# An eighth weight chunk by seven block products, the last mix's preparation moved ahead, and one ring of banks, in a float32 kernel on one Trainium2 core

## The reference, cut to what matters

```
u = rms_norm(x, norm_in_g)
proj = u @ w_in                      # 1024 x 4096: 16 chunks of 256 columns
pool_x, pool_z, m_x, m_z = split(proj)   # chunks 0-3, 4-7, 8-11, 12-15
pooled_g = window_mean(pool_x[g], w) - pool_x[g]     # w = 2, 4, 8, 16
mixed_g = pooled_g @ pool_w[g]                       # 256 x 256
y_pool = mixed * pool_scale * silu(pool_z)
h = x + y_pool @ w_out[:1024] + y_m @ w_out[1024:]
```

## Time and profile before

| | |
|---|---|
| median of 3 runs | 1152.65 us (1152.45 to 1152.68) |
| profiled execution, time | 1152.89 us |
| its span | 1151.1 us |
| PE busy | 1140.1 us, 99% of the span |
| DVE, ACT, POOL busy | 63%, 34%, 42% |
| granted TensorE clock | 0.998 |

### The profile page before, as it was taken

The page is one execution under the profiler, slowest core; times in us unless marked ns, Lnnn a source line. Parts: engine busy times, 40 slices in busy tenths (PEclk is TensorE's granted clock), DMA queues, the critical chain, the costliest instruction groups (busy, mean ns, idle before and its releaser), DMA issues.

```text
span 1151.1 us, 17423 instructions
## 1 busy us (share of the span) xinstructions
PE 1140.1 (99%) x6515; PEld 931.5 (81%) x6515; DVE 727.4 (63%) x1335; ACT 386.5 (34%) x758; POOL 482.7 (42%) x475
## 2 busy tenths in 40 slices
PE   9999999999999999999999999999999999999997
PEld 6888887888888887788888888889888887777786
DVE  5944545467344894467777964894698434556668
ACT  7432233222000022546574621341111134553422
POOL 2356655332223241244666765304224224455534
PEclk9999999999999999999999999999999999999999
DMA  8323343213325522101114241232111220142113
GB/s 245 120 64 121 99 146 104 90 51 114 110 67 193 209 69 97 52 24 28 47 42 161 64 175 45 102 124 74 43 50 38 66 71 1 38 149 101 44 40 138
DMA packets 84230, 104.07 MB, mean 90 GB/s; under 512 B 14258, under 2 KB 61578, under 8 KB 82995
## 3 DMA queue, kind: packets, MB, share of 16 engines
q1 hardware_dynamic: 76422, 99.21, 25.9%
q10 hardware_dynamic: 7724, 3.74, 1.2%
HBM read 80.35 MB, written 24.17 MB: 91 GB/s over the span
## 4 chain that ended last, share of the span: by engine, by line
PE 86%; POOL 8%; DMA 3%; ACT 1%; issue 1%; DVE 1%; POOLq 0%; DVEq 0%; ACTq 0%
PE bank L1064 20%; PE bank L1066 19%; PE bank L1065 19%; PE bank L1394 4%; POOL wlo L845 4%; PE bank L1369 4%; DMA wraw<-in_w_in 3%; PE wide L1385 2%; PE wide L1594 2%; PE bank L1333 1%; PE bank L1322 1%; PE bank L1310 1%; PE wide L1066 1%; PE wide L1065 1%; PE wide L1064 1%
## 5 line engine op out<-in xcount | busy, mean ns | idle before, releaser
L804 POOL CAST whi<-wraw 128x2048 fp32r<-128x2048 f32 x24 | 48.0, 1999 | 334.6 <-PE bank L1066 267.3
L1064 PE MATMUL bank<-x_hi,wlo 128*128 128x512 f32 x312 | 123.6, 396 | 0.0
L1064 PE MATMUL bank<-u_hi,wlo 128*128 128x512 f32 x308 | 120.6, 392 | 1.4 <-POOL wlo L808 1.4
L1066 PE MATMUL bank<-x_hi,whi 128*128 128x512 f32 x312 | 121.7, 390 | 0.0
L1065 PE MATMUL bank<-x_lo,whi 128*128 128x512 f32 x312 | 121.7, 390 | 0.0
L1066 PE MATMUL bank<-u_hi,whi 128*128 128x512 f32 x308 | 120.0, 390 | 0.0
L1065 PE MATMUL bank<-u_lo,whi 128*128 128x512 f32 x308 | 120.0, 390 | 0.0
L808 POOL TENSOR_TENSOR wlo<-wraw,whi 128x2048 fp32r<-128x2048 f32 x21 | 99.8, 4750 | 2.1 <-ACT whi L2908 0.5
L1064 PEld LDWEIGHTS bank<-x_hi,wlo 128*128 128x128 f32 x312 | 58.6, 188 | 16.1 <-issue 4.3
L1008 POOL TENSOR_SCALAR sp<-sp,rcx 128x384 f32<-128x384 f32 (+1 forms) x64 | 37.9, 606 | 76.4 <-DVE rcx L2392 76.3
L1064 PEld LDWEIGHTS bank<-u_hi,wlo 128*128 128x128 f32 x308 | 57.9, 188 | 14.8 <-POOL wlo L808 1.8
(11 more groups left out here) (431 smaller groups left out, 2846.4 us busy)
## 6 DMA issues: line engine op xcount, KB each, us to landing
wraw<-in_w_in SPq DMA_DIRECT2D x19, 1024.0 KB, 5.4
wraw<-in_w_out SPq DMA_DIRECT2D x12, 1024.0 KB, 5.4
wraw<-in_w_in SPq DMA_DIRECT2D x16, 512.0 KB, 4.8
xr<-in_x SPq DMA_DIRECT2D x8, 512.0 KB, 6.8
hst<-in_x SPq DMA_DIRECT2D x4, 1024.0 KB, 5.2
hpool<-hst SPq DMA_DIRECT2D x4, 1024.0 KB, 4.2
h<-hpool SPq DMA_DIRECT2D x4, 1024.0 KB, 7.0
resid<-h SPq DMA_DIRECT2D x8, 512.0 KB, 2.6
```

The costliest lines, as they stand in the source:

```text
L804: g_.tensor_copy(whi[w % 2][:, :, :], wraw[:, :, :]).then_inc(s["w_hi"], 1)
L1064: pe.matmul(ps, al, bh, start=(k == 0), stop=False)
L1066: return pe.matmul(ps, ah, bh, start=False, stop=(k == nk - 1))
```

## The change

Three things. (1) The last gates (chunk 7 of w_in) join the seven-product chunks: `SEVEN` has eight numbers, 2 to 9, the gates are stored to DRAM and come back by a third `load_sz`. P1 to P3 get the numbers 10 to 12 in place of 9 to 11; OP0 is still 13. The low part of P1's weights is now made by DVE (`BY_VECTOR`, `low_w`), inside the `add_up` of the last seven-product chunk. (2) On DVE both windows and the low parts of mix 3 come ahead of `mixed(2)`, and the first four results of OP0 are taken out between `mixed(2)` and `mixed(3)`. (3) OP0's last four groups use `ring_g` too.

```diff
-    plan = [("w_in", c, "f") for c in (0, 12, 8, 9, 10, 13, 6, 5, 4, 1, 2, 3, 7)]
+    plan = [("w_in", c, "f") for c in (0, 12, 8, 9, 10, 13, 7, 6, 5, 4, 1, 2, 3)]
...
-SEVEN = range(2, 9)
+SEVEN = range(2, 10)
...
-    W_POOL, W_SZ3, W_OP, W_MX, W_MZ, W_OM, W_2 = (0, 9, 10, 11), 12, 13, 14, 16, 20, 24
+    W_POOL, W_OP, W_MX, W_MZ, W_OM, W_2 = (0, 10, 11, 12), 13, 14, 16, 20, 24
-    BY_VECTOR = (W_MZ + 2, W_MZ + 3, W_OM, W_OM + 1)
+    BY_VECTOR = (W_POOL[1], W_MZ + 2, W_MZ + 3, W_OM, W_OM + 1)
...
@@ SP
-            wt(W_SZ3)
+            wt(W_OP)
             load_sz(2)
-            wt(W_OP)
...
             for q in range(2):
                 load_h(0, q)
+            load_sz(3)
             wt(W_OP + 2)
@@ PE
-            for i in range(4):
-                group(W_SZ3, i, u_hi, u_lo, "a_sz", 8 + i + 1)
...
-                          ps=ring_x("v_hp", n) if q == 0 and i >= 4 else None)
+                          ps=None)
@@ DVE
                 if c == N7 - 1:
                     ve.wait_ge(s["g_blk"], 4 * N7)
+                    low_w(W_POOL[1])
                     low_mix(0)
                 add_up(c, 4)
                 add_up(c, 5)
...
-            for g in (2, 3):
-                window(g, 0)
-                mixed(g - 1)
-                window(g, 1)
-                low_mix(g)
+            window(2, 0)
+            mixed(1)
+            window(2, 1)
+            low_mix(2)
+            for m in range(2):
+                window(3, m)
+            low_mix(3)
+            mixed(2)
...
+            for n in range(4):
+                empty_out(n)
             mixed(3)
@@ ACT
+                if g == 3:
+                    high_px(g, 1)
                 for n in range(4 * g - 4, 4 * g):
                     high_y(n)
-                if g == 3:
-                    ac.wait_ge(s["v_yr"], 12)
-                    for i in range(4):
-                        m, nh = i // 2, i % 2
-                        ps = filled(ac, "t_gemm", first[W_SZ3] + i + 1, "a_sz", 8 + i + 1)
-                        ac.activation(sz[:, m, nh * HALF:(nh + 1) * HALF], ps[:, :], ACT.Silu).then_inc(s["a_sz"], 1)
```

More of the change, by code:

```diff
@@ L173, in build @@
     um_d = nc.dram_tensor("umraw", [P, 6, S], F32).ap()
-    sz_d = nc.dram_tensor("szpool", [P, 2, 2, S], F32).ap()
+    sz_d = nc.dram_tensor("szpool", [P, 3, 2, S], F32).ap()
     row_t = nc.dram_tensor("relr", [8, RELS], F32)
@@ L377, in build @@
         early = {
-            "l_sz": ("l_h0", 32), "l_um0": ("l_h1", 16), "l_um1": ("l_h2", 16), "l_um2": ("l_h3", 16),
+            "l_sz": ("l_h0", 48), "l_um0": ("l_h1", 16), "l_um1": ("l_h2", 16), "l_um2": ("l_h3", 16),
             "o_st0": ("l_kB", 16 * (N7 - 1)), "o_st1": ("l_ln", 16 * (N7 - 1)),
@@ L590, in load_sz @@
                 sp_.wait_ge(s["o_st1"], 16 * (N7 - 1))
-                sp_.dma_start(sz[:, :, :], sz_d[:, 2 - g, :, :]).then_inc(s["l_sz"], 16)
+                sp_.dma_start(sz[:, :, :], sz_d[:, 3 - g, :, :]).then_inc(s["l_sz"], 16)
             for f in range(2):
@@ L1791, in window, with low_w @@
                 ve.wait_ge(s["v_px"], 5 * g + m + 1)
+            def low_w(w):
+                ve.wait_ge(s["w_hi"], high_count(w))
+                ve.tensor_tensor(wlo[w % 2][:, :, :], wraw[:, :, :], whi[w % 2][:, :, :].bitcast(F32),
+                                 ALU.subtract).then_inc(s["w_lo"], 1)
             def low_mix(g):
@@ L1803, in mixed @@
             def mixed(g):
-                if g in (1, 2):
+                if g:
                     ve.wait_ge(s["l_sz"], 16 * g)
                 else:
-                    ve.wait_ge(s["a_sz"], 8 + 4 * (g == 3))
+                    ve.wait_ge(s["a_sz"], 10)
                 for i in range(5):
@@ L1874, in _, with empty_out @@
             low_mix(1)
-            for g in (2, 3):
-                window(g, 0)
-                mixed(g - 1)
-                window(g, 1)
-                low_mix(g)
+            window(2, 0)
[6 more added lines that the diff above has]
+            mixed(2)
+            def empty_out(n):
+                q, t = n // NT, n % NT
+                if q % 2:
+                    ve.wait_ge(s["v_hp"], n - 7)
+                else:
+                    ve.wait_ge(s[f"l_xh{t // 4}"], 16 * (q // 2 + 1))
+                ps = filled(ve, "t_gemm", first[W_OP + q] + t + 1, "v_hp", n + 1)
+                ve.tensor_tensor(hst[:, t, :], ps[:, :], hst[:, t, :], ALU.add).then_inc(s["v_hp"], 1)
+            for n in range(4):
+                empty_out(n)
             mixed(3)
@@ L1949, in _ @@
                             fold_keys(t - 6)
[L1950 to L1955, removed]
+                    if n >= 4:
+                        empty_out(n)
                     if n >= 26:
                         conv_steps(2)
[L1958 to L1962, removed]
             conv_steps(8)
@@ L2685, in _ @@
                 high_px(g, 0)
+                if g == 3:
+                    high_px(g, 1)
                 for n in range(4 * g - 4, 4 * g):
                     high_y(n)
-                if g == 3:
-                    ac.wait_ge(s["v_yr"], 12)
-                    for i in range(4):
-                        m, nh = i // 2, i % 2
-                        ps = filled(ac, "t_gemm", first[W_SZ3] + i + 1, "a_sz", 8 + i + 1)
-                        ac.activation(sz[:, m, nh * HALF:(nh + 1) * HALF], ps[:, :], ACT.Silu).then_inc(s["a_sz"], 1)
-                high_px(g, 1)
+                if g < 3:
+                    high_px(g, 1)
             for n in range(12, 16):
```

## The result

| | before | changed |
|---|---|---|
| median | 1152.66 us (6 runs) | 1162.28 us (1161.90 to 1163.86, 6 runs) |
| ratio | | 1.0083, 95% interval 1.0071 to 1.0095 |
| profiled execution, time | 1152.89 us | 1163.86 us |
| its span | 1151.1 us | 1162.1 us |

The change makes the kernel 9.6 us slower. Forecast were 6.65 us, 1159.3, in a range that ended at 1161.8: right in direction, too small, and the measured time lies outside the range. The profiled execution of the changed kernel was the slowest of its six, 1.58 us above their median; the before's lay 0.23 above its own.

A forecast was written before the change was run, and what follows sets the result against it. The prediction took PE, busy 99% of the span, as the bound. It summed +4.80 us (first place and removed work), +1.55 and +0.3 (second place) to +6.65, giving 1159.3 us against the median, range 1156.5 to 1161.8.

The forecast's parts named there:

- Removed work: Block products on PE: seven take 84 matmuls for 96, 12 x 0.2267 = 2.72 us less.
- First place, the chain: At P1: cast after the last product, low part, low_mix(0), two add_up; wait 9.05 us, with the removed work +4.80 us.
- The rival in which P1's cast is released early: At P1: cast released three products before the end, no wait there; 1148.4 to 1150.3 us, chance 0.03.
- every new wait of PE is paid in full: On PE, whose longest wait was 1.4 us: each new wait adds its length, each matmul staying at 0.2267 us.
- Second place: P3 to OP1: POOL's split of OP1's weights lengthens window(3, 1), delaying PE by 1.55 us and 0.3 us.
- Window 5.87 us longer: window(3, 1) on DVE, beside POOL's cast and subtraction: forecast to end at 288.0 and not at 282.1.
- `mix(3)`: On PE behind OP0's first 48 matmuls: forecast to start 1.55 us late, waiting for the first result of mixed(2).
- fifth group of OP0: On PE: needs bank0, so the first empty_out, at 297.4 against 297.14; 0.3 us late.
- The wait of OP1: On PE at OP1: gates ready at 307.0 to 309.3, OP1 due at 308.3; taken as 0, 1.0 for the range.
- the gates' landing: The gates' return behind two transfers of hst: landing 5.2 to 7.5 us after the issue, at 300.5 to 302.8.

The follow-up runs named there:

- e9: The kernel before with the low part of P1's weights made by DVE, behind the fourth add_up of the last seven-product chunk; 1151.38 us, ratio 0.9986.
- e7: The changed kernel with the edits of e5 and e6 together; 1148.57 us, ratio 0.9965.
- e3: The changed kernel with the blocks placed by place(b) = b % 8 in place of (b + 2) % 8; 1153.67 us, ratio 1.0009.
- e2: The changed kernel with DVE's low part of P1's weights moved behind low_mix(0) and the fifth and sixth add_up; 1158.45 us, ratio 1.0045.
- e5: The kernel of e3 with the fifth and sixth add_up ahead of low_mix(0) on DVE; 1151.53 us, ratio 0.9994.
- e1: The changed kernel with 36 matmuls, their result read by nobody, added on PE behind the last block product; 1160.59 us, ratio 1.0064.
- e8: The changed kernel with mixed(2) moved back between window(3, 0) and window(3, 1); 1168.32 us, ratio 1.0135.
- e6: The changed kernel with POOL's split of OP1's weights held until four results of OP0 are taken out; 1159.08 us, ratio 1.0059.
- e4: The changed kernel with the low part of P1's weights left on POOL, as in the kernel before; 1160.33 us, ratio 1.0061.

## Why the prediction was right in direction and too small

**Removed work: right.** PE has 6503 matmuls for 6515. e9 against e7 gives 2.3 to 2.8 us for them, 2.72 was the sum's term.

**First place, the chain: right.** A wait of 9.05 us at P1 was forecast and 9.05 measured, with the cast, the subtraction, `low_mix(0)` and both `add_up` where they were put. e3 shows that the pair holds the cast, e2 that the queue behind the subtraction costs 4.46 of the 9.05, e5 that without both P1 does not wait. The rival in which P1's cast is released early did not occur; it is what e3 makes.

**The step that failed: "every new wait of PE is paid in full".** It was paid for more than in full. I priced the wait by its length and took every matmul behind it at 0.2267 us, though the clock of before, 0.998, is that of an engine that never stood still for more than 1.4 us. In the 8.9 us at P1 the granted clock fell to half, and the matmuls behind them cost 2.2 us that no term of the sum held. e1 shows that this is the clock and nothing else there: with PE kept busy the clock stays at 1.00 and the slow matmuls are gone. With the price measured here the sum would have given 1159.3 + 2.2 = 1161.5, and moved the range with it.

e1's time fell by 1.7 us (1.4 when each kernel is taken against before's median in its own session), where 2.2 to 2.4 was expected. How much the fall costs differs from one execution to the next. Behind the same wait of 8.9 us it was 1.8 us in e8's profile, 2.2 in the changed kernel's and 2.5 in e6's. The clock was back 3.7, 4.6 and 5.3 us behind P1's first matmul: each us that the matmuls ran at half cost 0.47 to 0.48.

The Trainium skill states the rule ("TensorE: Matmul & The Clock Gate", section "Part 1: The HAM clock gate"): the clock follows how busy TensorE was of late, and an idle one falls to 1.2 GHz. The traces here agree: 0.50 in the changed kernel from 219.30, while PE stood still, and 1.00 in e1, where it was kept busy.

**Second place: right in mechanism, one term too small.** Window 5.87 us longer (5.9), `mix(3)` 1.6 late, 1.7 with its slower first matmul (1.55), fifth group of OP0 0.3 (0.3). e6 shows that POOL's split is what lengthens the window, and that all three waits hang on it. The wait of OP1 was taken as 0 with 1.0 in the range, and was 1.15 in the profiled execution; in five other profiles with the same second place it lay between 0.25 and 1.2. The step behind it was the gates' landing, for which I had chosen 5.2 us after the issue: behind the two halves of `hst` it took 7.8 (324.71 to 332.5). In the five others it took 6.9 to 7.8, and the wait went with it: 0.25 and 0.34 us where it took 6.9 and 7.0 (e2, e1), 0.7 to 1.2 where it took 7.4 to 7.8 (e3, e5, e4). My upper end, 7.5, was the landing of the second of two such transfers; this was the third in a row. The choice of the lower one was wrong.

**The sum once more.** +4.80 (first place and removed work), +1.8 to 2.5 (clock, behind a wait of this length), +1.7, +0.3, and 0.3 to 1.2 for OP1: 8.9 to 10.5, and measured 9.6. In the profiled execution PE was 0.6 us later than in before at 41 us already, and 0.2 more at the first block product, which is part of why its own difference, 11.0, is larger than that of the medians. That part lies ahead of the stretch and is not the change's: in its first 20 us PE waited 0.6 us for the transfer of `hot` and 0.5 for DVE, waits that before's view does not have, and other profiles scatter in the same way. The last matmul of the block products starts between 214.54 (e6) and 217.62 (e4, with its fallen clock at the start), where 215.63 is the changed kernel's and 214.78 was forecast.

**Left open.** Whether a wait between 2.6 and 4.4 us lets the clock fall was not tried. Nor do the runs show why the clock comes back 3.7 us behind P1's first matmul in one execution and 5.3 in another, or why it fell at the start of e4's alone.

## What to carry to other kernels

When a wait of several microseconds is created on an engine that never waited, price what follows it too: look for the granted clock behind the longest waits. When work is moved to a faster engine, price what is queued behind it there, not its own duration: here 2.3 us on DVE cost PE 2.2 us more than 4.5 us on POOL, and the same move was a gain where the bank was released ahead of it. And when a chunk number shifts by one, walk through everything that goes by its parity; here one line that turns the blocks' places by two quarters was worth 8.6 us.

## What the runs showed of the hardware

TensorE stood still for 2.6 us and kept its clock (e3), and after 4.4, 5.6, 6.7 and 8.9 us it ran at half (e2, e8, e4, the changed kernel). That is no rule for safe waits: at the start of e4's profile, where PE had sparse work and no wait above 1.2 us, the clock was at 0.50 from 9.3 to 12.7 us.

What came after a fall cost 1.5 to 2.9 us in slow matmuls (0.43 us apart for 0.23), and did not grow with the wait: 2.5 us behind 4.4, 2.9 behind 5.6, 1.5 behind 6.7, and 1.8, 2.2 and 2.5 behind 8.9. It went with the stretch from the first matmul to the clock's return: 3.1 us in e4, 3.7 and 6.1 in e8, 4.6 in the changed kernel, 5.3 in e2 and e6, at 0.47 to 0.49 us for each.

DVE's steps with two inputs in SBUF and POOL's steps took turns, and the window's lengthening came out as forecast (5.87 us for 5.9): a step of 1.26 us took 5.54 beside a subtraction of POOL in before and 5.55 in the change. A step of DVE that reads PSUM was not held: 0.75 us beside the cast in before, and two in 1.41 us beside the subtraction in e6.
